# VectorE takes 41 instead of 30 of the 128 rows of V that each position adds up: a hybrid attention and expert kernel on one core

## What is computed

```
q = (c @ w_query) ...; s1, i1 = top_k(...); s2, i2 = top_k(...); top, sel = top_k(s1 + s2)
idx = take_along_axis(cidx, sel);  g = softmax(top)
u = expert_u[idx]
act = gelu(einsum('td,thkd->thk', c, u))
coef = (g * act)
return einsum('thk,thkd->td', coef, expert_v[idx])
```

## Time and profile before

| | |
|---|---|
| median of 3 runs (range) | 4390.84 us (4384.69 to 4396.41) |
| the profiled execution itself | 4385.67 us, its span 4384.0 us |
| TensorE clock granted, mean | 0.912 of full |
| busy: TensorE, VectorE, ScalarE, GpSimd | 3443.2, 2834.4, 1181.7, 2759.3 us |
| dot products L1410 | 1152, 1405.2 us |
| adds on VectorE L1424 | 278, 357.3 us (nine more, the first of each position, are L1421) |
| row matmuls L789 | 3460 (865 rows), 1840.0 us |
| gathers L660 (U), L671 (V) | 1152 and 1152, 1369.1 and 1337.1 us |

### The profile page before, as it was taken

The page is one execution under the profiler, slowest core; times in us unless marked ns, Lnnn a source line. Parts: engine busy times, 40 slices in busy tenths (PEclk is TensorE's granted clock), DMA queues, the critical chain, the costliest instruction groups (busy, mean ns, idle before and its releaser), DMA issues.

```text
span 4384.0 us, 33556 instructions
## 1 busy us (share of the span) xinstructions
PE 3443.2 (79%) x9668; PEld 1653.3 (38%) x9668; DVE 2834.4 (65%) x5497; ACT 1181.7 (27%) x2303; POOL 2759.3 (63%) x2364
## 2 busy tenths in 40 slices
PE   8998546877796787779687878877887777868877
PEld 3444323433342343344244334433442333323333
DVE  1121266686768768776876787687778554587775
ACT  0100314213312421441154135313531332111111
POOL 0000017777777777787777777777677544667875
PEclk9999678998899999999999998999999898989998
DMA  4111319999999999999999999999999887899996
GB/s 170 60 53 58 142 58 379 369 349 368 391 337 364 370 357 356 372 353 347 362 361 351 333 350 347 348 352 358 347 354 353 309 283 270 325 367 377 369 377 226
DMA packets 448998, 1355.99 MB, mean 309 GB/s; under 512 B 47296, under 2 KB 117824, under 8 KB 447808
## 3 DMA queue, kind: packets, MB, share of 16 engines
q0 software_dynamic: 333072, 1212.83, 74.4%
q1 hardware_dynamic: 115760, 141.21, 9.3%
HBM read 1325.54 MB, written 28.31 MB: 309 GB/s over the span
## 4 chain that ended last, share of the span: by engine, by line
PE 31%; POOL 24%; DMA 13%; issue 10%; DVE 9%; ACT 4%; SPq 0%; ACTq 0%; POOLq 0%; DVEq 0%
PE sum_ps L789 15%; POOL v_rows L671 12%; POOL u_rows L660 11%; PE z_ps L732 8%; DMA v_rows<-expert_v_in,idx_tile 6%; DMA u_rows<-expert_u_in,idx_tile 6%; DVE u_rows L1410 2%; PE z_ps L809 1%; DVE neg_max L1571 1%; PE z_ps L919 1%; DVE arena L1501 1%; PE out_ps L836 1%; ACT diag L1139 1%; PE z_ps L892 1%; DMA qd<-qk_turned 1%
## 5 line engine op out<-in xcount | busy, mean ns | idle before, releaser
L789 PE MATMUL sum_ps<-v_rows,diag 128*128 128x512 f32 x3460 | 1840.0, 669 | 619.2 <-DMA v_rows<-expert_v_in,idx_tile 396.3
L1410 DVE CUSTOM_DVE_ANT_0 u_rows<-u_rows,c_rows 128x1024 f32<-128x1024 f32 x1152 | 1405.2, 1225 | 624.5 <-DMA u_rows<-expert_u_in,idx_tile 608.7
L660 POOL DMA_INDIRECT u_rows<-expert_u_in,idx_tile x1152 | 1369.1, 1188 | 646.2 <-issue 313.2
L671 POOL DMA_INDIRECT v_rows<-expert_v_in,idx_tile x1152 | 1337.1, 1161 | 351.3 <-issue 317.8
L789 PEld LDWEIGHTS sum_ps<-v_rows,diag 128*128 128x128 f32 x3460 | 669.8, 209 | 1517.2 <-issue 853.0
L1139 ACT ACTIVATE diag<-ident,coef 128x128 f32<-128x128 f32 x865 | 312.8, 394 | 636.1 <-PE sum_ps L789 571.7
L142 PE MATMUL proj_ps<-weights,aT 128*128 128x512 f32 x864 | 378.5, 596 | 9.9 <-ACT aT L171 9.9
L1424 DVE SCALAR_TENSOR_TENSOR acc<-v_rows,coef,acc 128x1024 f32<-128x1024 f32 x278 | 357.3, 1285 | 10.7 <-DMA v_rows<-expert_v_in,idx_tile 10.6
L732 PE MATMUL z_ps<-w_query_sb,arena 128*128 128x512 f32 x576 | 255.4, 597 | 1.1 <-ACT arena L1101 1.1
L142 PEld LDWEIGHTS proj_ps<-weights,aT 128*128 128x128 f32 x864 | 162.9, 191 | 207.3 <-issue 195.1
L125 POOL TENSOR_TENSOR stat<-stat,minus_half 128x1 f32<-128x1 f32 x9 | 5.0, 557 | 338.5 <-DVE stat L193 338.5
(11 more groups left out here) (176 smaller groups left out, 3120.2 us busy)
## 6 DMA issues: line engine op xcount, KB each, us to landing
u_rows<-expert_u_in,idx_tile POOLq DMA_INDIRECT x1152, 6.5
v_rows<-expert_v_in,idx_tile POOLq DMA_INDIRECT x1152, 6.5
weights<-w_in_in SPq DMA_DIRECT2D x6, 2048.0 KB, 19.8
qk_turned<-turned SPq DMA_DIRECT2D x36, 256.0 KB, 2.8
w_out_sb<-w_out_in SPq DMA_DIRECT2D x2, 4096.0 KB, 18.7
w_query_sb<-w_query_in SPq DMA_DIRECT2D x1, 8192.0 KB, 28.7
x<-x_all_in POOLq DMA_DIRECT2D x9, 512.0 KB, 3.7
arena<-x_all_in SPq DMA_DIRECT2D x9, 512.0 KB, 7.1
```

What stands on the lines that cost most here:

```text
L660: pool.indirect_dma_start(u_rows[r % U_RING][:, :], None, ins["expert_u"], bass.IndirectOffsetOnAxis(ap=idx_tile[:, e % 2, at:at + 1], axis=0)
L671: pool.indirect_dma_start(v_rows[g % V_RING][:, :], None, ins["expert_v"], bass.IndirectOffsetOnAxis(ap=idx_tile[:, e % 2, at:at + 1], axis=0)
L789: mm = nc.tensor.matmul(sum_ps[:, half * W:(half + 1) * W], diag[:, by_tensor[g] % DIAGS, :], v_rows[g % V_RING][:, half * W:(half + 1) * ...
L1410: nc.vector.tensor_tensor_reduce(row, row, c_rows[e % 2][:, :], 1.0, 0.0, ALU.mult, ALU.add, dots[:, s % 2, r % TOP:r % TOP + 1]).then_inc ...
```

## The change

Only the lists in `vector_rows` change. Rows that VectorE takes in steps 0 to 7:

| position | before | now |
|---|---|---|
| 0 to 4 | 5, 4, 4, 4, 4, 4, 2, 0 | 7, 6, 7, 7, 6, 5, 4, 2 |
| 5, 6 | 5, 5, 5, 5, 4, 4, 2, 0 | 7, 6, 7, 7, 6, 5, 4, 2 |
| 7 | 7, 5, 7, 7, 4, 4, 2, 0 | 7, 5, 7, 7, 6, 5, 4, 2 |
| 8 | unchanged | unchanged |

Step 0 of position 0 has no rows of V yet. In all VectorE takes 405 rows instead of 287, and TensorE 747 instead of 865.

```diff
@@ vector_rows
     if e == TP - 1 and s < 4:
         return (7, 9, 11, 12, 14) if s == 1 else (1, 3, 5, 7, 9, 11, 13)
-    if s == 0:
-        return (2, 5, 8, 11, 14)
     if s == 1:
-        return (7, 9, 11, 12, 14) if e > 4 else (7, 9, 11, 14)
+        return (6, 8, 10, 11, 13, 14)
     if s < 4:
-        return (2, 5, 8, 11, 14) if e > 4 else (2, 6, 10, 14)
-    return ((2, 6, 10, 14), (2, 6, 10, 13), (6, 13), ())[s - 4]
+        return (1, 3, 6, 8, 10, 12, 14)
+    return ((1, 4, 6, 9, 11, 14), (2, 5, 8, 11, 14), (3, 7, 10, 13), (6, 13))[s - 4]
```

## The result

The changed kernel is slower by 0.3%: 4399.03 us against 4387.06 us (medians of 12 runs each, alternating), ratio 1.0031, 95% interval 1.0017 to 1.0045, or +13.6 us (7 to 20). The time lies inside the predicted range; the sign was wrong. Twelve runs of each tell this 0.3% from nothing, which the text ahead of the prediction had put just out of reach. Its title is off, too: 405 and 287 rows over nine positions are 45 instead of 32 of the 128 rows of a position.

A forecast was written before the change was run, and what follows sets the result against it. No engine is full: issue of gathers paces most steps, elsewhere TensorE, step 4's series or VectorE. A to F sum to -13 - 5 - 14 + 10 + 5 + 3 = -14 us, so 4377 us, range 4340 to 4412.

The forecast's parts named there:

- A: Attention steps of positions 5 and 6: 14 rows leaving TensorE shorten VectorE's waits for scores, net of added adds; -13 us.
- B: Position 4 and first attention steps of positions 2 to 4: the same wait for scores, in small, shortens; -5 us.
- C: Steps 4 and 5, positions 0 to 7: a row leaves TensorE's series of heads, w_out and norm; -14 us.
- D: Step 7, positions 0 to 7: row 6's add stands between VectorE's gapless passes and counts whole; +10 us.
- E: Steps 5 and 6: one more add in step 5 and row 10's add in step 6 partly count; +5 us.
- F: All gathers: 118 more adds that a gather can meet, at 0.025 us an add; +3 us.
- slower rival: Steps paced by gathers: adds hold gathers up, deciding above about 0.15 us an add; 4411 us, chance 0.16.
- Full relief: Late attention and steps 4 and 5: each row off TensorE counts whole; -42 us, 4349 us, chance 0.20.
- Nothing: Gathers set the pace almost everywhere; steps 5 to 7 take back what C and A gain; 4391 us, chance 0.22.
- clock rival: TensorE with fewer rows gets a lower clock, so the gains of A and C go; 4400 us, chance 0.05.

The follow-up runs named there:

- e_attend: Kernel before with the changed lists in steps 0 to 3 alone; 1.0008, +3.5 us against before.
- e_best: Changed kernel with VectorE's rows in step 6 moved to 1, 3, 5, 7 and in step 7 to 11 to 14; 1.0012, +5 us against before.
- e_norow0: Kernel before (its attention lists kept) with steps 4 to 7 as in e_best; 0.9977, -10 us against before.
- e_s4: Kernel before with the changed list of step 4 alone; 0.9964, -16 us against before.
- e_row0: Kernel before with e_best's steps 4 to 7, and row 0 on VectorE in steps 0, 2, 3 of positions 4 to 6; 0.9971, -13 us against before.
- e_combo: Kernel before with row 0 on VectorE in positions 4 to 6 and rows 11 to 14 in step 7; 0.9983, -7 us against before.
- e_swap: Changed kernel without its 118 surplus rows: before's number of adds in each step, at the changed places; 0.997, -13 us against before.
- e_s4_swap: e_swap with all six adds of the changed list in step 4; 0.9948, -23 us against before, 4361.3 us.
- e_short: Changed kernel with its 118 surplus adds covering only 32 of 1024 columns; 0.9935, -28 us against before.
- e_short_zero: e_short with TensorE also adding products with zeros for 113 of the rows it lost; 0.9941, -26 us against before.
- e_zero: Changed kernel with TensorE adding products with zeros for 113 of the 118 rows it lost; 1.0029, +13 us against before.
- e_s7_mid: Kernel before with rows 4 to 7 of step 7 moved to VectorE, in the middle of its passes; 1.0063, +28 us against before.
- e_s7_end: Kernel before with rows 11 to 14 of step 7 moved to VectorE, behind its passes; 0.9968, -14 us against before.
- e_mid: Kernel before with the changed lists in steps 4 and 5 only; 0.9989, -5 us against before.
- e_place: Changed kernel with VectorE's rows in step 6 moved to 1, 3, 5, 7 and in step 7 to 12, 14; 1.0001, 0 us against before.

## Why the prediction was right or wrong

**A and B (-18): no gain, the step that failed.** e_attend, which has this part alone, gives +3.5 us (-2 to +9), and e_best against e_norow0, which also differ in it alone, +15. Attention steps of positions 4 to 6, us in the profiles:

| adds in attention | kernels | sum |
|---|---|---|
| before's number and places | 8 (e_s4 and e_norow0 among them) | 626.6 to 635.1, mean 630.5 |
| the same with 11 adds more, row 0 | e_row0, e_combo | 623.5, 626.6 |
| changed | 6 | 629.0 to 644.1, mean 639.2 |
| before's number, changed places | e_swap, e_s4_swap | 628.6, 634.9 |
| changed, surplus short | e_short, e_short_zero | 626.9, 620.0 |

The changed lists cost 9 us there in the mean instead of gaining. (The lowest of the six, 629.0, is e_attend's, whose profiled execution was 17 us under its median.) Position 6 shows most of it. Its four attention steps before, after and in e_swap (columns as in the earlier trace rows):

```profile
2993.50:3210.90 217.40, 179.96 (x681) 102.14 (x680) 172.83 (x218) 113.63 (x168) 153.50 (x127) 0.93 0.95 345
```

```profile
2997.50:3221.60 224.10, 178.21 (x652) 102.62 (x651) 180.96 (x225) 111.74 (x161) 156.88 (x128) 0.89 0.94 336
```

```profile
2980.90:3196.30 215.40, 178.02 (x681) 101.61 (x681) 172.96 (x218) 113.66 (x168) 155.38 (x127) 0.94 0.96 345
```

Seven adds more are 8.1 us more of VectorE (172.83 to 180.96), and the stretch is 6.7 us longer; TensorE's 29 recorded matmuls fewer bring 1.8 us at the lower clock. e_swap has the work of before and nearly its length. In position 4, before and after, the clock stays and TensorE gets its relief, 11.2 us, yet the stretch is no shorter:

```profile
2172.40:2376.40 204.00, 166.03 (x611) 95.28 (x610) 154.55 (x214) 102.07 (x174) 162.37 (x127) 0.92 0.97 356
```

```profile
2177.30:2381.70 204.40, 154.80 (x574) 90.36 (x573) 166.13 (x224) 99.25 (x164) 161.54 (x126) 0.91 0.96 354
```

Position 5 is alike: TensorE's busy time fell by 12.4 us at a clock of 0.90 in both, the stretch from 213.8 to 211.5 us.

The prediction's reading was that two waits of VectorE for scores are TensorE's. In positions 5 and 6, of which A speaks, the waits ahead of the four maxima were 18.4, 0, 40.7 and 2.5 us and are 22.7, 0, 27.5 and 9.2. The third fell by 13, more than the 7 that I took; the fourth rose by 7 (predicted 10, and "late next" was right). The first, at which I expected -8.6, rose by 4. Over positions 0 to 6 all four together rose from 107 to 109 us while VectorE got its adds on top. My reading, argued from this and not tested by itself: a wait in a loop of two engines isn't a surplus of the one waited for; both are on the path by turns, and an add lengthens it where a row had lain beside it. GpSimd's account of positions 4 to 6 says the same: its gathers took 475.7 us and take 482.1, its waits for dot products 50.6 and 56.7, the short gaps between gathers 107.9 and 102.7. It waits for VectorE, nowhere long for TensorE. That TensorE's row is worth nothing, its clock included, is shown twice, within some 10 us each: e_zero against the changed kernel and e_short_zero against e_short.

**C (-14): right in size, its mechanism not shown.** e_s4 alone gives -16 us (-21 to -10). The series did get shorter: in the mean of eight positions from the first transpose of the heads to w_out 2.37 us instead of 3.35 (predicted 1.0 less), from w_out to the transposes of the tokens 7.55 instead of 8.42 (predicted 0.75), the whole of it 26.14 instead of 27.39 us. But the signs of a shorter path are weak. The wait ahead of L1471 fell by 3.2 us over nine tiles (62.1 to 58.9), not by 1 us each. GpSimd's wait for the tokens' norm is 51.2 us after and 52.7 in e_s4 for 53.3. Step 4, which I expected 1 to 2 us shorter a position, takes over eight positions 442.6 us after and 445.2 in e_s4 for 443.8; only in the mean of eleven kernels with the changed list (439.7) and six with the old one (445.9) is it 0.8 us shorter a position. And in e_zero the series is as long as before (27.61 us) at no cost against the changed kernel. What is shorter in e_s4 is step 5, 398.2 us over eight positions, and so it is in e_swap (397.7), in which TensorE's load is that of before; it was 404.1 before and 400.0 to 409.0 in six kernels with both old lists. So the gain can be one of places as well as of the rows that left TensorE. For the rows speaks e_s4_swap against e_swap, two rows a position: -10 us, uncertain by as much. This stays open.

**D (+10): right.** Step 7 takes 391.2 us before and 402.7 after (+11.5); e_s7_mid prices an add there at 1.29 us and e_s7_end at nothing behind the passes.

**E (+5): too small.** I took 0.35 us for the add in step 5; e_mid against e_s4 gives 1.5 us a position, +12 (+11 by the runs). It took back most of C's gain.

**F (+3): right as a mean, wrong as a model.** The mean of the two kinds of gather went from 1.175 to 1.180 us, under the 1.19 that I set for the slower rival (that of U alone is 1.199). But 118 adds cost 0.36 us each (e_short), above the 0.15 at which that rival decides. It isn't a price that each add pays to the gathers: it is 1.29 in the middle of step 7, about 1.5 in step 5, nothing at the end of step 7.

The sum with what was measured: A and B +9, C -16, step 5 +12, steps 6 and 7 +13.5, together about +18, against +13.6 (7 to 20) measured. One size ahead of the sum was wrong as well: 118 rows were to take 203 to 300 us from TensorE (2.7 us a row would even make it 317), and its busy time fell by 105 us, partly because the mean matmul got slower.

**The rivals.** Full relief falls: TensorE's relief gives nothing. "Nothing" had its bookkeeping right (what step 4's list gains, step 5 takes back through VectorE) and its size too kind. The slower rival was nearest, in sign and as to which engine; its place, every step paced by gathers, was wrong. Attention in positions 0 to 3 is such a place: gathers and the short gaps between them fill 710 of GpSimd's 730.5 us before. Yet it took 730.5 us in the mean of the kernels with the old lists and 730.5 with the changed ones, with 38 adds more. This also fits the reading that those steps aren't set by TensorE. The clock rival named something real, since the clock fell from 0.912 to 0.884 and ate the relief in position 6. It isn't the cause of the loss: positions 4 and 5 kept their clock and gained nothing to speak of, e_zero has 0.903 and +13 us, e_short 0.892 and -28.

**Open.** Of the 28 us that e_short gains, 13 are the places (e_swap). The other half may be ScalarE's 118 diagonals or the short adds' rhythm; e_short_zero excludes TensorE and no more. Why the changed places are better than the old at equal number isn't known; the profiles put it mostly in step 5. The pieces don't add up (e_best against e_place and e_s7_end, e_combo), which the intervals of 4 to 10 us partly cover. And no run tries a limit by DMA: its share is 0.90 to 1.03 in the windows shown, and every kernel moves the same rows, so a faster issue of gathers might meet it at once.

## What to carry to other kernels

Price an instruction by its place, not by its engine's mean share: with VectorE busy 68% overall, an add cost its whole duration in a run without gaps and nothing in the waits for rows to land (the end of step 7, attention in positions 0 to 3). Beside a wait for an engine that waits in turn for this one, as in the late attention steps, it wasn't free. A visible wait for an engine doesn't show that relieving that engine helps; put its load back as dummy work, and one run tells what relief and clock are worth together. Where one list sets many steps, change them one by one: one step's gain of 16 us was hidden here under its neighbour's loss.

## What the runs showed of the hardware

A gather's duration on GpSimd follows VectorE closely. In the profile before, a gather that began while VectorE was idle took 0.94 us (598 of them), 901 that began during a dot product took 1.36 us in the mean and, where they were held, ended 0.81 us after it, and 265 that began in an add took 1.04. Instructions of VectorE with one input, or with an input from PSUM, didn't hold it (0.94 us). This agrees with the Trainium skill, "SBUF — State Buffer", section "Who interferes with whom", that the one that comes second waits. It also shows why an add is cheaper than a dot product, though it holds a gather just as long: 18 gathers that began 0.2 to 0.4 us into an add took 1.75 us. An add stands right behind a dot product, and a gather held by that ends 0.81 us after it, so that the next one, 0.30 us later, meets only the end of the add: 178 of the 265 began over 1.0 us after the add's start.

TensorE's granted clock fell from 0.912 to 0.884 when 14% of the rows left it, and a recorded matmul on a row of V took 707 ns for 669: part of what is taken from it, it loses again.
